# Three edits to a fused two-block transformer layer on one core: the last norm's root, its closing banks, and the place of the second norm's late transposes

## The reference

```python
def rmsnorm(x, g):
    x32 = x.astype(jnp.float32)
    y = x32 * lax.rsqrt(jnp.mean(x32 * x32, axis=-1, keepdims=True) + NORM_EPS)
    return (y * g.astype(jnp.float32)).astype(x.dtype)
...
def second_block(...):
    for layer in range(DEPTH_2):
        h = rmsnorm(x, mix_norms[layer])
        if layer % 2 == 0:
            x = x + rwkv_attention_mixer(h, *mix_params[layer])
        else:
            x = x + conformer_conv(h, *mix_params[layer])
        g_ffn, up, down = ffn_params[layer]
        x = x + sq_relu_mlp(rmsnorm(x, g_ffn), up, down)
    return rmsnorm(x, final_norm)
```

## Time and profile before

| | us |
|---|---|
| median of three runs | 970.25 (968.92 to 970.41) |
| the profiled execution | 971.87 |
| its span, from the first to the last instruction | 970.1 |
| PE busy | 924.7 (95%) |
| DVE busy | 642.0 (66%) |
| ACT busy | 455.5 (47%) |
| POOL busy | 74.4 (8%) |
| mean granted clock of TensorE | 0.986 |

### The profile page before, as it was taken

How to read it: one execution, slowest core, us unless ns; L and a number is a source line. 1 busy time by engine, 2 the same in 40 slices (tenths; PEclk the granted TensorE clock), 3 DMA queues, 4 the chain that set the end, 5 groups by cost and what they waited for, 6 DMA issues and landing times.

```text
span 970.1 us, 15398 instructions
## 1 busy us (share of the span) xinstructions
PE 924.7 (95%) x6352; PEld 794.1 (82%) x6352; DVE 642.0 (66%) x853; ACT 455.5 (47%) x651; POOL 74.4 (8%) x151
## 2 busy tenths in 40 slices
PE   6999999999999999999899999999998899999995
PEld 4888788899799988878688888888974688888884
DVE  5579788678768875736476656666756766666663
ACT  6445555444658344421364454445433655444441
POOL 6000000000210040000000000000653000000000
PEclk9999999999999999989999999999999899999998
DMA  9755444555664621000156655565882346665521
GB/s 324 242 184 170 148 156 142 172 199 184 199 200 157 217 87 45 1 1 5 42 174 215 195 197 174 181 208 150 251 241 56 112 155 199 209 198 190 174 87 43
DMA packets 105941, 152.42 MB, mean 157 GB/s; under 512 B 4098, under 2 KB 82448, under 8 KB 105872
## 3 DMA queue, kind: packets, MB, share of 16 engines
q1 hardware_dynamic: 101424, 141.45, 44.5%
q0 software_dynamic: 4272, 9.85, 3.8%
q10 hardware_dynamic: 176, 0.14, 0.0%
HBM read 145.58 MB, written 1.06 MB: 151 GB/s over the span
## 4 chain that ended last, share of the span: by engine, by line
PE 89%; DVE 6%; ACT 2%; issue 2%; DMA 0%; POOL 0%; DVEq 0%; POOLq 0%; SPq 0%; ACTq 0%
PE banks L1932 21%; PE banks L1885 14%; PE banks L1886 14%; PE banks L1887 13%; PE banks L1933 10%; PE banks L2272 4%; PE banks L2477 2%; DVE wl L1077 1%; PE banks L2360 1%; PE banks L2044 1%; PE banks L2068 1%; PE banks L1994 1%; PE banks L2371 1%; PE banks L2033 1%; PE banks L2366 1%
## 5 line engine op out<-in xcount | busy, mean ns | idle before, releaser
L1077 DVE TENSOR_TENSOR wl<-raw,wh 128x2048 fp32r<-128x2048 f32 x130 | 297.7, 2292 | 113.5 <-ACT wh L653 113.0
L653 ACT ACTIVATE wh<-raw 128x2048 fp32r<-128x2048 f32 x132 | 252.1, 1912 | 138.6 <-PE banks L1887 96.2
L1932 PE MATMUL banks<-x,wh 128*128 128x512 f32 x896 | 314.8, 394 | 0.0
L1933 PE MATMUL banks<-x,wl 128*128 128x256 f32 x896 | 250.5, 280 | 0.0
L1932 PEld LDWEIGHTS banks<-x,wh 128*128 128x128 f32 x896 | 168.2, 188 | 39.5 <-issue 3.0
L1933 PEld LDWEIGHTS banks<-x,wl 128*128 128x128 f32 x896 | 168.4, 188 | 1.2
L1885 PE MATMUL banks<-wh,yh 128*128 128x512 f32 x288 | 114.6, 398 | 3.0 <-DVE yl L1633 3.0
L1887 PE MATMUL banks<-wh,yl 128*128 128x512 f32 x288 | 113.4, 394 | 0.0
L1886 PE MATMUL banks<-wl,yh 128*128 128x512 f32 x288 | 113.2, 393 | 0.0
L1885 PE MATMUL banks<-x,wh 128*128 128x256 f32 x320 | 91.8, 287 | 1.7 <-DVE x L1145 1.5
L1886 PE MATMUL banks<-x,wh 128*128 128x256 f32 x320 | 89.9, 281 | 0.0
(11 more groups left out here) (364 smaller groups left out, 1247.1 us busy)
## 6 DMA issues: line engine op xcount, KB each, us to landing
raw<-in_l_ffn_up SPq DMA_DIRECT2D x32, 1024.0 KB, 5.5
raw<-in_l_ffn_down SPq DMA_DIRECT2D x32, 1024.0 KB, 5.0
raw<-in_w_in SPq DMA_DIRECT2D x29, 1024.0 KB, 5.3
raw<-in_l_w_in SPq DMA_DIRECT2D x13, 1024.0 KB, 5.2
raw<-in_l_pw SPq DMA_DIRECT2D x12, 1024.0 KB, 5.7
arena<-arena POOLq DMA_DIRECT2D x64, 71.0 KB, 3.8
raw<-in_w_out SPq DMA_DIRECT2D x4, 1024.0 KB, 5.1
raw<-in_l_w_out SPq DMA_DIRECT2D x4, 1024.0 KB, 5.0
```

The costliest lines, as they stand in the source:

```text
L653: nc.scalar.activation(wh[:, u % WBUFS, :], raw[:, u % RAWS, :], ACT.Copy).then_inc(E("hi_split"), 1)
L1077: nc.vector.tensor_tensor(wl[:, u % WBUFS, :], raw[:, u % RAWS, :], wh[:, u % WBUFS, :].bitcast(F32), ALU.subtract).then_inc(E("lo_split"), 1)
L1932: mm(outs[t], h[:, k, c], x2[:, k, :, :].rearrange("p w t -> p (w t)"), start=k == 0, stop=False)
L1933: ins = mm(outs[t][:, 0:T], l[:, k, c], xh[:, k, :], start=False, stop=k == KC - 1)
```

## The change

Three edits stand together.

1. *Root.* The last norm's root is no longer POOL's power: ACT takes a square root with the other sums as bias, DVE the reciprocal. ACT runs one small Sqrt ahead, behind the last MLP step, and POOL's last instruction becomes the load of the gain. ACT also scales the last 512 columns of the second row half and stores them from its own queue; SP stores the other three pieces, and waits for that store too.
2. *Banks.* In `f1`, the second to last `D` unit does three of its four banks; bank (1,1) gets its share of that unit between the banks (0,1) and (1,0) of the last unit and is closed there. The last unit's share for it goes into two narrow banks of 256 columns, `end0` and `end1`, which are closed last. DVE adds them with `end_add`.
3. *Transposes.* The late transposes of `n2` move from behind the projection into unit `rw6`, behind its first 12 matmuls. For the MLP `f0` the code is written anew with the same order of work.

```diff
--- before.py
+++ after.py
@@ -111,7 +111,7 @@
            ("Z1", "act"), ("EZ", "act"), ("ZZ", "dve")]
 
 
-OUT_PIECES = ((0, 0, DM), (1, 0, DM // 2), (1, DM // 2, DM))
+OUT_PIECES = ((0, 0, DM // 2), (0, DM // 2, DM), (1, 0, DM // 2))
 HEAD_TURNS = {3 * n + 1: n for n in range(10)}
 
 
@@ -261,7 +261,10 @@
                 if i == FF_STEPS:
                     for b in range(4):
                         s.use(f"dn{tag}_{b}", 4 + b)
-                s.unit("D", down, 256 * (i - 1), 0, f"dn{tag}_3" if i == FF_STEPS else None)
+                    if tag == "f1":
+                        s.use("end0", 0), s.use("end1", 1)
+                last = {"f0": (None, "dnf0_3"), "f1": ("dnf1_3", "end1")}[tag]
+                s.unit("D", down, 256 * (i - 1), 0, last[i - FF_STEPS + 1] if i >= FF_STEPS - 1 else None)
 
     ffn("f0", "l0_ffn_up_2", "l0_ffn_down_2")
     norm("n4")
@@ -521,6 +524,7 @@
                 sp.wait_ge(E("out_ready"), n + 1)
                 sp.dma_start(out_d[0, s * P:(s + 1) * P, a:b], xn[:, s, a:b]).then_inc(E("out_stored"), 16)
             sp.wait_ge(E("out_stored"), 16 * len(OUT_PIECES))
+            sp.wait_ge(E("end_stored"), 16)
 
 
         @block.gpsimd
@@ -626,7 +630,6 @@
             pool.wait_ge(E("ln_lo"), 5)
             pool.dma_start(gfin, bass.AP(tensor=A["final_norm_2"].tensor, offset=0, ap=[[0, P], [1, DM]]))\
                 .then_inc(E("gain_loaded"), 16)
-            rows_rstd()
 
 
         @block.scalar
@@ -1049,7 +1052,31 @@
             for _ in range(4):
                 next_unit()
             ffn("f1", FF_STEPS, "pw")
-            squares("dnf1")
+            mark(nc.scalar.activation(NMAX[:, 0:1], EPSL, ACT.Sqrt))
+
+            def end_square(use, t, a, b, total):
+                wait_empty(act, use)
+                nc.scalar.activation(scratch[:, t * DM + a:t * DM + b], xn[:, t, a:b], ACT.Square, scale=DM ** -0.5,
+                                     accum_out=total).then_inc(E("end_squares"), 1)
+
+            def end_root(t, last, squares):
+
+                act.wait_ge(E("end_squares"), squares)
+                act.wait_ge(E("end_others"), t + 1)
+                nc.scalar.activation(RSTD[:, t:t + 1], last, ACT.Sqrt, bias=MS[:, t:t + 1]).then_inc(E("end_rooted"), 1)
+
+            end_square("dnf1_0", 0, 0, 512, SS[:, 0:1])
+            end_square("dnf1_1", 0, 512, DM, SS[:, 1:2])
+            end_root(0, SS[:, 1:2], 2)
+            end_square("dnf1_2", 1, 0, 512, SS[:, 2:3])
+            end_square("end0", 1, 512, 768, SS[:, 3:4])
+            end_square("end1", 1, 768, DM, SSG[:, 0:1])
+            end_root(1, SSG[:, 0:1], 5)
+            act.wait_ge(E("end_gained"), 1)
+            act.wait_ge(E("end_rstd"), 2)
+            nc.scalar.activation(xn[:, 1, 512:DM], xn[:, 1, 512:DM], ACT.Copy, scale=RSTD[:, 1:2]).then_inc(E("end_scaled"), 1)
+            act.wait_ge(E("end_scaled"), 1)
+            act.dma_start(out_d[0, P:2 * P, DM // 2:DM], xn[:, 1, 512:DM]).then_inc(E("end_stored"), 16)
 
 
         @block.vector
@@ -1842,15 +1869,37 @@
                 nc.vector.scalar_tensor_tensor(out=xn[:, t, a:b], in0=xn[:, t, a:b], scalar=RSTD[:, t:t + 1],
                                                in1=gfin[:, a:b], op0=ALU.mult, op1=ALU.mult).then_inc(E("out_ready"), 1)
 
-            ffn_add("f1", 0, 0), ffn_add("f1", 0, 1)
-            mean_squares(0).then_inc(E("mean_square"), 1)
-            ffn_add("f1", 1, 0), ffn_add("f1", 1, 1)
-            rstd_of(0)
-            scale_out(0, 0, DM)
-            mean_squares(1).then_inc(E("mean_square"), 1)
-            rstd_of(1)
-            scale_out(1, 0, DM // 2)
-            scale_out(1, DM // 2, DM)
+            def end_add(n):
+
+                name, cols = f"end{n}", slice(512 + T * n, 512 + T * n + T)
+                wait_full(dve, name)
+                nc.vector.scalar_tensor_tensor(out=xn[:, 1, cols], in0=bank(name)[:, 0:T], scalar=RSQ[:, 1:2],
+                                               in1=xn[:, 1, cols], op0=ALU.mult, op1=ALU.add).then_inc(empty(name), 1)
+
+            def end_rstd(t):
+                dve.wait_ge(E("end_rooted"), t + 1)
+                nc.vector.reciprocal(RSTD[:, t:t + 1], RSTD[:, t:t + 1]).then_inc(E("end_rstd"), 1)
+                dve.wait_ge(E("end_rstd"), t + 1)
+
+            ffn_add("f1", 0, 0)
+            ffn_add("f1", 0, 1)
+            dve.wait_ge(E("end_squares"), 1)
+            nc.vector.tensor_scalar(MS[:, 0:1], SS[:, 0:1], 1e-6, None, ALU.add).then_inc(E("end_others"), 1)
+            ffn_add("f1", 1, 1)
+            end_rstd(0)
+            scale_out(0, 0, 512)
+            ffn_add("f1", 1, 0)
+            wait_empty(dve, "dnf1_3")
+            end_add(0)
+            end_add(1)
+            scale_out(0, 512, DM)
+            dve.wait_ge(E("end_squares"), 4)
+            nc.vector.tensor_scalar(MS[:, 1:2], SS[:, 2:3], SS[:, 3:4], 1e-6, ALU.add, ALU.add).then_inc(E("end_others"), 1)
+            wait_empty(dve, "end0"), wait_empty(dve, "end1")
+            dve.wait_ge(E("end_squares"), 5)
+            nc.vector.tensor_tensor(xn[:, 1, 512:DM], xn[:, 1, 512:DM], gfin[:, 512:DM], ALU.mult).then_inc(E("end_gained"), 1)
+            end_rstd(1)
+            scale_out(1, 0, 512)
 
 
         @block.tensor
@@ -2000,7 +2049,7 @@
                         nat_unit((f"{tag}{c}_0", f"{tag}{c}_1"), half, ah, al, None if c else source)
                         if norm and c and not half:
                             row_transposes(norm, tag, 0)
-                if norm:
+                if norm and norm != "n2":
                     row_transposes(norm, tag, 1)
 
             rows_scaled = [0]
@@ -2184,7 +2233,10 @@
                     give(ins, f"nat_{name}{tt}")
 
             for n, u in enumerate(RW_ORDER):
-                t_unit(f"rw{u}", None if n else "n2", halves=not n)
+                if n == 0:
+                    t_unit(f"rw{u}", "n2", halves=True, between=lambda: row_transposes("n2", "wo", 1))
+                else:
+                    t_unit(f"rw{u}")
                 if n == 0:
                     pe.wait_ge(E("row_diag"), NT)
                     give(mm(take("rb")[:, 0:T], const("ones"), row_diag, start=True, stop=True), "rb")
@@ -2432,6 +2484,36 @@
             row_transposes("f0", "wp", 1)
 
             def ffn(tag, k0):
+                def down(u, j, quarters):
+
+                    h, l = w_views(u, DM)
+                    pe.wait_ge(E("hidden_lo"), k0 + j + 1)
+                    buf = 2 * (j % 3)
+                    for s, c in quarters:
+                        b, name, rs = 4 + 2 * s + c, f"dn{tag}_{2 * s + c}", slice(s * P, (s + 1) * P)
+                        if j == 0:
+                            pe.wait_ge(emptied[b], PL.uses[name][1])
+                            seen[b] += 1
+                        last = FF_STEPS - 2 if (tag, s, c) == ("f1", 1, 1) else FF_STEPS - 1
+                        for k in range(2):
+                            cs = slice(512 * c, 512 * c + 512)
+                            ins = three(banks[:, b, :], yh[:, buf + k, rs], yl[:, buf + k, rs], h[:, k, cs], l[:, k, cs],
+                                        j == 0 and k == 0, j == last and k == 1)
+                        if j == last:
+                            give(ins, name)
+                    return ins
+
+                def narrow_end(u, j):
+
+                    h, l = w_views(u, DM)
+                    buf, rs = 2 * (j % 3), slice(P, 2 * P)
+                    for n in range(2):
+                        out, cs = take(f"end{n}")[:, 0:T], slice(512 + T * n, 512 + T * n + T)
+                        for k in range(2):
+                            ins = three(out, yh[:, buf + k, rs], yl[:, buf + k, rs], h[:, k, cs], l[:, k, cs], k == 0, k == 1)
+                        give(ins, f"end{n}")
+
+                rows_first, columns_first = [(0, 0), (0, 1), (1, 0), (1, 1)], [(0, 0), (1, 0), (0, 1), (1, 1)]
                 for i in range(FF_STEPS + 1):
                     if i < FF_STEPS:
                         wide_unit(f"up{tag}_{i}", None if i else tag)
@@ -2439,26 +2521,19 @@
                         continue
                     u, j = unit[0], i - 1
                     arrived(u)
-                    h, l = w_views(u, DM)
-                    pe.wait_ge(E("hidden_lo"), k0 + j + 1)
-                    buf = 2 * (j % 3)
-                    columns_first = tag == "f0" and j == FF_STEPS - 1
-                    for s, c in ((0, 0), (1, 0), (0, 1), (1, 1)) if columns_first else ((0, 0), (0, 1), (1, 0), (1, 1)):
-                        if columns_first and (s, c) == (1, 1):
-                            row_transposes("n4", "dnf0", 0)
-                        b = 4 + 2 * s + c
-                        if j == 0:
-
-                            pe.wait_ge(emptied[b], PL.uses[f"dn{tag}_{2 * s + c}"][1])
-                            seen[b] += 1
-                        for k in range(2):
```

(20 more changed lines are left out.)

## The result

| | before | after |
|---|---|---|
| median, five executions each in turn on one chip, us | 968.92 (967.12 to 970.41) | 962.45 (959.60 to 965.29) |
| ratio, 95% interval | | 0.9931 (0.9906 to 0.9957) |
| profiled execution, us | 971.87 | 959.60 |
| its span, us | 970.1 | 957.8 |
| its mean granted clock | 0.986 | 0.994 |

The change makes the kernel faster by 6.47 us, 0.69%; the forecast was 5.96 us, or a ratio of 0.9939. In microseconds the forecast was 964.3 with a range from 962.5, and 962.45 lies just under it. Slow executions, over 1.5% above the fastest of their kernel, are left out of all medians and ratios: one of the kernel before (5183 us), one of `banks_undone` (982.6 us) and the profiled one of `transposes_only` (987.6 us).

The account below looks back on a forecast made before the run. PE held 89% of the span, but POOL's drain alone held the last 4.8 us. Drain 4.8 + tail 0.3 + transposes 0.86 = 5.96, taking the median from 970.25 to 964.3 us; range 962.5 to 969.0.

Parts of the forecast that it names:

- The drain: At the block's end: with POOL's powers gone, its 9.1 us drain runs early and is hidden, gaining 4.8 us.
- the lower end of 3.2: At the block's end: the drain's gain if the profiler lengthens it by 1.6 us.
- Rival B: At the block's end: the gap moves with the last store, so only 1.2 us is gained, 969.1; chance 0.15.
- The transposes: In the second norm: late transposes inside `rw6` let `rb` start 0.86 us earlier, at 268.69; ends 0.4 and 1.34.
- I let the 0.86 through: Behind `rb`: later stretches follow PE, so the whole 0.86 us reaches the end.
- The tail: From PE's last matmuls to the last landing: reordered banks, root and stores gain 0.3 us; ends 0.9 gained, 0.6 lost.
- The landing: At the end: two 256 KB stores starting together land at 964.6, behind last scalings at about 961.75.
- ACT's table load: Before the last squares: the early Sqrt's load of 1.28 us falls in ACT's idle 5.39 us and costs nothing.
- rival D: At `end_root`: table loads between Square and Sqrt cost 2.2 us, with the drain's gap staying: 971.2; chance 0.04.
- C: At the end: drain hidden but another end takes its place, 2 to 4 us remain, 966 to 968; chance 0.05.
- The base: Whole kernel: the starting median of 970.25 us, from which the gain of 5.96 was subtracted.
- the same 7.0: Whole kernel: the largest gain, 4.8 + 1.34 + 0.9 = 7.0 us, giving 963.2 before the range was widened to 962.5.

Follow-up runs that it names:

- banks_undone: Kernel after with the last four banks wide again and both scalings of the first row half ahead of DVE's last add: 964.05 us, ratio 0.9955.
- transposes_only: Kernel before with only the late transposes of the second norm moved into the mixer's first unit: 968.11 us, ratio 0.9992.
- late_pool: Kernel after with a one-column POOL memset added behind the last sum of squares: 967.02 us, ratio 0.9988.
- drain_probe: Kernel before with four more drains on POOL's queue at places where POOL is idle, POOL's root kept: 964.26 us, ratio 0.9959.
- one_drain: Kernel before with one POOL drain added behind the load of the last gain, POOL's root kept: 964.03 us, ratio 0.9945.
- early_pool: Kernel after with a one-column POOL memset added when the first of the last banks is full: one execution, 963.91 us.
- after_again: Kernel after, unchanged, compared again with the kernel before on the same chip: 962.44 us against 969.31, ratio 0.9937.
- root_only: Kernel before with POOL's powers replaced by ACT's square roots and DVE's reciprocals; banks, stores and transposes as before: 963.82 us, ratio 0.9944.
- sp_store: Kernel after with the last output piece stored by SP instead of ACT: one execution, 961.73 us.
- sixteen_more: Kernel before with 16 more small transfers issued by POOL, 119 in all: an execution of 970.39 us.
- more_transfers: Kernel before with 32 more small transfers issued by POOL at 276 us, 135 in all: one execution, 970.46 us.
- banks_wide_interleaved: Kernel after with the last four banks wide again and DVE's last add between the scalings of the first row half: 963.43 us, ratio 0.9949.

## Why the prediction was right, and where it was wrong

**The drain: right.** 4.8 forecast, 4.9 read. One point of the step was left open in the prediction, whether the profiler lengthens the drain (the lower end of 3.2). Every execution on record comes with a recorded span and clock, so no run here is free of that. But the 1.6 us on which the 3.2 rested lie within the scatter of the kernel before (965.3 to 971.7 us), and by medians the root edit alone gives 4.9 us and one drain 5.3. The drain does wait for POOL's last load as well: right behind the issue it is 9.09, long behind it 8.6. And late_pool, drain_probe and one_drain show the cause to be POOL's queue, which rests on more than the 4.9 us alone. Rival B is false: nothing of the 4.9 moved with the last store. The Trainium skill ("Runtime: NRT & Kernel Launch", The ~15µs preamble/postamble breakdown) puts a barrier, a reset of semaphores and a reset of rings of about 1.5, 1.5 and 2 us behind the kernel, 5.0 in all. In this case the trace does not bear that out for the gap between SP's drain and the meeting, which is 0.1 us after the change. Between the span and the device time lie 1.8 us in both kernels (971.87 - 970.1 and 959.60 - 957.8), and no run here shows what is in them.

**The transposes: right.** The start of the late transposes was forecast at 263.0 and is 263.01 (262.9 without the drift of 0.13); the gain at `rb` 0.86, read 0.88. "I let the 0.86 through" holds about: 0.80 is what the split near 360 shows on the mean of the traces.

**The tail: the mechanism right, the size low.** Forecast 0.3, read 0.6. PE is not the reason: its last matmul starts 0.18 later, but is 0.28 long and not 0.39, so that it ends 0.07 later (14.46 against 14.39 us behind the split), "about where it ended". The handovers behind it were taken too long. On the clock of the trace before (6.81 us on, the distance between the two splits) the gain product ends at 960.55 (forecast 960.85) and the last scalings at 961.44 (961.75): 0.3 sooner. The prediction let DVE wait for the last sum of squares until 960.1, with 0.73 for a square with its sum where consecutive starts here are 0.63 apart, and 0.5 for a narrow one where they are 0.40 apart. The last sum stands at 959.7, and DVE's queue sets the start of the product, at 959.87. The three squares after, which the last sum closes:

```profile
951.39 0.63 ACT L1059 ACTIVATE arena<-xn 128x512 f32<-128x512 f32 x1 [1.83 <-DVE xn L1707]
...
952.02 0.40 ACT L1059 ACTIVATE arena<-xn 128x256 f32<-128x256 f32 x1
...
952.42 0.40 ACT L1059 ACTIVATE arena<-xn 128x256 f32<-128x256 f32 x1
```

The landing was near, 2.7 against the 2.85 of the working (961.75 to 964.6). ACT's table load, with PE still at work, was right as well; its two lines after are

```profile
943.24 1.28 ACT L1055 ACT_TABLE_LOAD   x1
944.54 0.20 ACT L1055 ACTIVATE small<-small 128x1 f32<-128x1 f32 x1
```

and no load follows them, so rival D is false. So is C: no other engine's drain is longer than SP's end allows (DVE's 0.79, ACT's 0.15, both over before 955.3).

**The sum.** By the traces it is 4.9 + 0.6 + 0.8 = 6.3 us, between the forecast of 5.96 and the medians' 6.47 and 6.87. The interval of the ratio in the second comparison spans 4.6 to 7.8 us, so 5.96, 6.3 and 6.87 are the same number for it.

**The base and the range: wrong.** The step that failed is the base of the sum, the median of 970.25, and with it the "half of the runs' spread of 1.5 us" by which the range was widened. The result is 1.8 us under the forecast of 964.3. Of this, 1.3 us is the base (970.25 against 968.92 in the comparison itself), and only 0.5 us the difference (6.47 against 5.96), 0.3 of it the tail's. The kernel before was executed 58 times beside the experiments: the median is 968.8, the lowest 965.3, the highest 971.7, and seven lie under 965.8. That is a spread of 6.4 us and not of 1.5. The three values at hand (968.92, 970.25, 970.41) lay in the upper half of that by chance. 968.8 - 5.96 = 962.8 would have been the forecast, and the range, with the same 7.0 and half of 1.5, would have begun near 961.

Where this scatter comes from can be read. Every execution comes with its mean granted clock. Of the 58, the six with 0.986 have a median of 970.2 us, the fifteen with 0.988 of 970.2, the sixteen with 0.989 of 968.7, the twelve with 0.991 of 966.4. A share of 0.005 more clock over 968 us is 4.8 us, and from 0.986 to 0.991 the medians fall by 3.8. Something else has a part in it: the sixteen with 0.989 reach from 966.0 to 969.3. In the traces the losses that differ stand between 350 and 500 us; one near 750 is in all of them (3.3 or 3.4 us in the sense below, and 5.1 in drain_probe). One window of each of three kernels, in the columns of the earlier trace rows (before, after, early_pool; late_pool's is like that of before, at 0.67):

```profile
420.00:430.00 10.00, 8.23 (x79) 6.70 (x77) 4.43 (x10) 1.08 (x2) 0.00 (x0) 0.71 0.01 2
```

```profile
420.00:430.00 10.00, 9.22 (x144) 7.24 (x144) 4.77 (x13) 1.08 (x2) 0.00 (x0) 1.00 0.01 2
```

```profile
420.00:430.00 10.00, 9.21 (x108) 7.18 (x105) 3.10 (x8) 1.08 (x2) 0.00 (x0) 0.66 0.01 2
```

The third number from the end is the clock, a mean over the window of its two levels, 1.00 (2.4 GHz) and 0.50 (1.2 GHz): 0.71 before, 1.00 after, and 0.66 in early_pool, which is the kernel after with an instruction that POOL runs at 950 us. In the 10 us ahead of it PE was busy 10.00 in before, 9.02 in after and 9.01 in early_pool. So the same program up to there, with PE equally busy ahead, has the low stretch or has it not: the change is not what makes it. Summed over the 15 windows of 10 us from 350 to 500 (ten times one less the clock), the loss is 6.8 us in the profile of before, 1.7 in that of after, 3.4 in after_again, root_only, one_drain, banks_undone, sp_store and sixteen_more, 1.7 in drain_probe, 5.1 in early_pool and more_transfers, 5.2 in banks_wide_interleaved and 6.8 in late_pool. It comes in steps of about 1.7, with and without each of the three edits. That is also the other half of the 12.3 us between the two profiles: 6.3 are the change, and the profile of before is an execution with 5.1 us more of this loss than that of after, which leaves 0.9 of the 12.3 unexplained. Between the splits near 360 and 457 us the profile of after is faster by 4.6 (92.0 against 96.6 us), in work that the change does not touch. drain_probe, with none of the three edits, takes 92.0 there as well, and late_pool, with all three, 96.6. What decides whether an execution has a low stretch stays open.

## What to carry to other kernels

Look at the drains of the block's end by engine before any edit of the last work: an engine that issued many transfers of its own may set the end long after its last useful instruction, and one early drain in its idle time is enough to take that away. An order on DVE near the end is worth more than the width of a bank: in this kernel the last add held up by 1.4 us cost 1.25 at the end, and the narrow banks gave 0.45. And take a base from the granted clock as well as from the median: three executions of one kernel that agree within 1.5 us can all lie on the same side of a scatter of 6.

## What the runs showed of the hardware

- POOL's drain costs about 0.08 us for each transfer that POOL has issued since its last drain: 0.67 with none, 6.39 with 66, 9.09 with 103, 10.40 with 119. About 0.5 of each is the load or power just ahead of it, for which it waits (8.6 with 103 and only a small memset ahead). It also waits for transfers still on their way (13.3 us at the program's start).
- Behind the 128th transfer of POOL stands a stop of 0.19 us, and the next drain is shorter than the count says (9.67 with 135).
- SP's and ACT's queues hand over 256 KB stores in 2.0 and 2.7 us at the end of this kernel; ACT's starts together with one of SP's.
- Twelve matmuls of 256 columns in place of six of 512: the last one starts 0.18 us later and ends 0.07 later (ends of matmuls are modelled in the trace).
- The granted clock of one program had its low stretches at other places and in another number from one execution to the next: 1.7 to 6.8 us of loss between 350 and 500 us in these traces, in steps of about 1.7.
